# Five barriers between dense stages taken out, with the next stage's first products split by token tile

## The reference

```python
x = x + mix @ w_out                                    # mix_out
hf = causal_dwconv(rms_norm(x, norm2_g) @ w_up, ...)   # up, 1024 -> 2 x 2816
gt, val = split(hf)
x = x + (gelu(gt) * val) @ w_down                      # down
gate = sigmoid(rms_norm(x, norm3_g) @ w_pg)            # gate
x = x + (p @ w_pe) * gate
x = rms_norm(x, final_g)
# second block, layer 0 (even): its input product, attention, experts
x @ even_w_in                                          # even_in
x = layer_norm(ALPHA * x + attention @ w_o, ...)
x = layer_norm(ALPHA * x + routed_moe(x), ...)         # combine0
# layer 1 (odd)
x @ odd_w_in                                           # odd_in
```

## Time and profile before

| | |
|---|---|
| median of 3 runs | 2108.26 us (2101.0 to 2108.62) |
| the profiled execution | 2099.9 us, its span 2098.1 us |
| mean granted TensorE clock | 0.956 of full speed |
| PE busy | 1959.4 us, 93% of the span |
| DVE busy | 671.2 us, 32% |
| ACT busy | 401.1 us, 19% |
| POOL busy | 82.0 us, 4% |
| moved by DMA | 335.56 MB, mean 160 GB/s |

### The profile page before, as it was taken

One profiled execution on the slowest core, in us unless ns is written; L12 is line 12 of the kernel. 1 busy time (PEld: TensorE's weight loads), 2 busy tenths in 40 slices (PEclk: granted clock), 3 DMA queues, 4 the chain that ended last, 5 costly groups with the idle time before them and its releaser, 6 DMA issues.

```text
span 2098.1 us, 23209 instructions
## 1 busy us (share of the span) xinstructions
PE 1959.4 (93%) x9718; PEld 879.6 (42%) x9718; DVE 671.2 (32%) x1600; ACT 401.1 (19%) x869; POOL 82.0 (4%) x106
## 2 busy tenths in 40 slices
PE   7999999999999988999996999998998997999997
PEld 3464444444444444444544333233644445333332
DVE  4736321223200223015534000014776635200005
ACT  3213011111100003105601111112125521111111
POOL 0000010000000000000001100010000000200001
PEclk9989999999999999998996999999989997999999
DMA  4103552221221122201135999992110243799995
GB/s 157 63 21 111 195 195 80 80 74 42 75 80 60 60 80 94 80 1 41 47 139 176 325 399 397 395 390 89 41 40 1 81 161 125 219 397 396 398 388 203
DMA packets 140633, 335.56 MB, mean 160 GB/s; under 512 B 4536, under 2 KB 12744, under 8 KB 140400
## 3 DMA queue, kind: packets, MB, share of 16 engines
q1 hardware_dynamic: 126384, 283.80, 37.3%
q0 software_dynamic: 10976, 37.76, 4.8%
q10 hardware_dynamic: 3168, 12.50, 1.5%
HBM read 310.94 MB, written 23.09 MB: 159 GB/s over the span
## 4 chain that ended last, share of the span: by engine, by line
PE 85%; DMA 6%; DVE 5%; ACT 2%; issue 1%; DVEq 0%; another core or an unknown queue 0%; ACTq 0%; SPq 0%
PE psum L582 39%; PE psum L982 20%; PE psum L825 7%; DMA ring<-in_moe_w_up 5%; PE psum L762 4%; PE psum L894 3%; PE psum L923 2%; PE psum L907 2%; PE psum L1076 1%; PE psum L963 1%; PE psum L594 1%; PE psum L704 1%; ACT ring L1434 1%; PE psum L1007 0%; PE psum L658 0%
## 5 line engine op out<-in xcount | busy, mean ns | idle before, releaser
L982 PE MATMUL psum<-ring,scratch 128*32 128x512 f32 x3840 | 515.5, 603 | 12.8 <-DMA ring<-in_moe_w_up 9.8
L582 PE MATMUL psum<-xT,ring 128*128 128x512 f32 (+2 forms) x1056 | 465.0, 601 | 8.5 <-PE psum L582 3.5
L582 PEld LDWEIGHTS psum<-xT,ring 128*128 128x128 f32 (+2 forms) x1056 | 199.4, 190 | 271.6 <-issue 270.7
L982 PEld LDWEIGHTS psum<-ring,scratch 128*32 128x32 f32 x3840 | 142.8, 111 | 299.0 <-issue 294.8
L582 PE MATMUL psum<-ring,xT 128*128 128x512 f32 (+4 forms) x704 | 240.2, 498 | 2.5 <-ACTq L1185 1.6
L582 PEld LDWEIGHTS psum<-ring,xT 128*128 128x128 f32 x704 | 120.4, 194 | 120.4 <-issue 112.2
L825 PE MATMUL psum<-ring,scratch 128*128 128x512 f32 x352 | 152.7, 594 | 4.0 <-remote 3.3
L1598 DVE SCALAR_TENSOR_TENSOR scratch<-psum,overlay,scratch 128x511 f32<-128x511 f32 x88 | 65.9, 749 | 230.8 <-ACT scratch L1364 229.3
L982 PE MATMUL psum<-xT,scratch 128*32 128x512 f32 x768 | 130.1, 606 | 9.6 <-DMA ring<-in_moe_w_up 9.6
L2135 DVE TENSOR_TENSOR scratch<-psum,scratch 128x512 f32<-128x512 f32 x24 | 16.6, 691 | 337.0 <-PE psum L982 337.0
L762 PE MATMUL psum<-xT,ring 128*128 128x512 f32 x224 | 103.0, 616 | 2.5 <-DVEq L1587 2.3
(11 more groups left out here) (374 smaller groups left out, 1650.4 us busy)
## 6 DMA issues: line engine op xcount, KB each, us to landing
ring<-in_moe_w_gate SPq DMA_DIRECT2D x28, 2048.0 KB, 15.6
ring<-in_moe_w_up SPq DMA_DIRECT2D x28, 2048.0 KB, 18.4
ring<-in_moe_w_down SPq DMA_DIRECT2D x24, 2048.0 KB, 15.1
ring<-in_w_up SPq DMA_DIRECT2D x11, 2048.0 KB, 7.9
xT<-in_moe_w_down SPq DMA_DIRECT2D x8, 2048.0 KB
expert_rows<-scratch ACTq DMA_DIRECT2D x20, 512.0 KB, 7.3
ring<-in_w_down SPq DMA_DIRECT2D x4, 2048.0 KB, 7.8
ring<-in_even_w_in SPq DMA_DIRECT2D x4, 2048.0 KB, 7.8
```

Source lines behind the costliest of these rows:

```text
L582: mm = nc.tensor.matmul(out_, lhsT, rhs, start=(j == 0), stop=(j == len(pairs) - 1))
L982: mm = nc.tensor.matmul(bank[r, :], lhsT[:, t, r], w_[:, t, c0:c0 + 512], start=(t == 0), stop=(t == nk - 1))
```

## The change

NO_MEET gets five stages more: mix_out, up, down, gate and combine0, so the barriers behind them are gone. In their place:

- up, even_in and odd_in begin with enter_features. It waits until tile 2 is in xT, does product 0 for the first 384 tokens, turns tile 3, does product 1 for 384 tokens, waits for tile 3 in xT and does both products for the last 128 tokens. turn_behind leaves tile 3 to it in mix_out, down and gate; combine turns three tiles only.
- down begins as soon as its weights and the first eight hidden tiles are there; each of its first four products waits for one of DVE's last four convolutions.
- gate begins with tile 0 when that is in xT, and turns tile 3 behind its first pair. Its pairs of banks start at bank 4 (gate_bank).
- the stages get semaphores of their own that are never cleared (out_mm, out_used, gate_mm, gate_opened, gate_used, late_taken); static and expert loads into a slot share one semaphore. The remaining Flow sets are cleared behind norm1 and even_in.
- GpSimd now waits in gate for the end of down, then for tile 3, ahead of its two loads, and in odd_in for the late sums ahead of its clearing. Its zero fill, pT load and the memset of qB no longer stand behind barriers.

```diff
-NO_MEET = ("even_out", "route0", "experts0", "overflow0", "odd_out", "route1", "experts1", "overflow1")
+NO_MEET = ("mix_out", "up", "down", "gate", "combine0", "even_out", "route0", "experts0", "overflow0", "odd_out", "route1", "experts1", "overflow1")
...
-        flow = {s: turns[i % 2] for i, s in enumerate(STAGES)}
+        flow = {"norm1": turns[0], "up": turns[1], "even_in": turns[0], "odd_in": turns[1], "latent": turns[0]}
+        done_with = {"norm1": turns[0:1], "even_in": turns}
...
+        def gate_bank(i):
+            return (2 * i + 4) % 8
...
                     turn_tile(stage, n - 1)
+                    if stage in ("mix_out", "down", "gate"):
+                        return
...
+            def tile_there(stage, n):
+                pe.wait_ge(tile_taken, norm_base[stage] + n + 1)
+                if stage == "combine0":
+                    pe.wait_ge(late_taken, n + 1)
+
+            def enter_features(behind, f, columns):
+                def part(k, q):
+                    w_, c0, m = columns[k]
+                    return product(banks[k][0:m, q], [(w_[:, t, c0:c0 + m], xT[:, t, q]) for t in range(KD)])
+                early, last = slice(0, (NT - 1) * P), slice((NT - 1) * P, T)
+                tile_there(behind, NT - 2)
+                part(0, early)
+                turn_tile(behind, NT - 1)
+                part(1, early)
+                tile_there(behind, NT - 1)
+                for k in range(2):
+                    part(k, last).then_inc(f.mm, 1)
...
             def down():
...
+                    pe.wait_ge(val_scaled, k0 + c[2])
                     for n in range(NT):
+                        if j == 0:
+                            pe.wait_ge(F["up"].v, 2 * FT - 3 + n)
...
             def gate():
...
+                        i = NT * half_ + n
+                        if half_ == 0:
+                            tile_there("down", n)
+                        else:
+                            pe.wait_ge(gate_used, i - NT + 1)
...
+                        if i == 0:
+                            turn_tile("down", NT - 1)
...
             def gate():
+                pool.wait_ge(out_mm, OUT_MM["down"] + 24)
                 pool.dma_start(rowsG, w["final_g"]).then_inc(rows_loaded, 16)
+                pool.wait_ge(tile_taken, norm_base["down"] + NT)
                 pool.dma_start(pack_area["even"], w["pack_even"]).then_inc(pack_loaded["even"], 16)
...
             def odd_in():
+                pool.wait_ge(late_done, NT)
                 clear_halves(kI)
```

More of the change, by code:

```diff
@@ L265, in build @@
         met = sem("met")
-        w_loaded = [sem(f"w_loaded{s}") for s in range(RING)]
+        w_loaded = [sem(f"w_loaded{s}") for s in range(RING + 1)]
         w_used = sem("w_used")
@@ L317, in build @@
         for l in range(2):
+            for b in slot_of[len(chunk_loads):first_expert_chunk[l]]:
+                buffer_loads[b] += 1
+                chunk_loads.append(buffer_loads[b])
             holder = {b: (i - RING - 1, None) for i, b in enumerate(FIRST_FREE[l])}
@@ L452, in build @@
         y_taken = sem("y_taken")
-        expert_loaded = [sem(f"expert_loaded{b}") for b in range(RING + 1)]
         y_stored = [sem("y_stored0"), sem("y_stored1")]
@@ L471, in turn_bank @@
         def turn_bank(stage, n):
-            return 2 * n if stage in ("gate", "combine0") else 2 * (n % 2)
+            if stage == "gate":
+                return gate_bank(n)
+            return 2 * n if stage == "combine0" else 2 * (n % 2)
+        def gate_bank(i):
+            return (2 * i + 4) % 8
         keys_cleared = sem("keys_cleared")
@@ L808, in up @@
                     w_ = slot_view(at, c)
-                    for g in range(4):
+                    if j == 0:
+                        enter_features("mix_out", f, [(w_, g * P, P) for g in range(2)])
+                    for g in range(0 if j else 2, 4):
                         k = 4 * j + g
@@ L865, in even_in @@
                     arrived(at)
+                    if j == 0:
+                        enter_features("gate", f, [(slot_view(at, c), g * P, P) for g in range(2)])
+                        k = 2
                     if j == 1:
@@ L971, in weights_of @@
                     b, loads = buffer_of[l][m, e]
-                    pe.wait_ge(expert_loaded[b], loads)
+                    pe.wait_ge(w_loaded[b], loads)
                     views.append(expert_buffer(b, 4 if m == "down" else KD))
@@ L1079, in combine @@
                 if l == 0:
-                    for n in range(NT):
+                    for n in range(NT - 1):
                         turn_tile("combine0", n)
@@ L1371, in gate @@
             def gate():
-                f = F["gate"]
                 def opened(i):
-                    act.wait_ge(f.mm, 2 * i + 2)
+                    act.wait_ge(gate_mm, i + 1)
                     if i >= 2:
-                        act.wait_ge(f.v, i - 1)
-                    A(gate_s[:, i % 2, :], banks[(2 * i + 1) % 8][:, :], ACT.Sigmoid).then_inc(f.a, 1)
+                        act.wait_ge(gate_used, i - 1)
+                    A(gate_s[:, i % 2, :], banks[gate_bank(i) + 1][:, :], ACT.Sigmoid).then_inc(gate_opened, 1)
                 for i in range(NT):
@@ L2329, in _, with meet @@
             steps = [2]
-            def meet(i):
+            def meet(stage):
                 meets[0] += 1
@@ L2335, in meet @@
                 pool.drain()
-                if i >= 0:
-                    f = turns[i % 2]
+                for f in done_with.get(stage, ()):
                     for s in (f.mm, f.a, f.v, f.s):
@@ L2488, in _ @@
             }
-            for i, s in enumerate(stages):
+            for s in stages:
                 if s in run:
@@ L2557, in load_experts @@
                             sp.wait_ge(met, meets_through("odd_d" if l else "even_ab"))
-                    sp.dma_start(expert_buffer(b, 4 if m == "down" else KD), views[m][e]).then_inc(expert_loaded[b], 16)
+                    sp.dma_start(expert_buffer(b, 4 if m == "down" else KD), views[m][e]).then_inc(w_loaded[b], 16)
             for at, c in static:
```

70 lines of the change are left out of this document (34 added, 36 removed).

## The result

| | before | after |
|---|---|---|
| median | 2105.65 us (2101.0 to 2108.62, 4 runs) | 2085.99 us (2083.75 to 2086.48, 4 runs) |
| ratio after / before | | 0.9907, 95% interval 0.9883 to 0.9930 |
| the profiled execution, its span | 2099.9, 2098.1 us | 2086.48, 2084.8 us |
| mean granted TensorE clock | 0.956 | 0.958 |
| PE busy | 1959.4 us | 1957.5 us |

A forecast was written before the change was run, and what follows sets the result against it. TensorE, busy in 93% of the span, bounds the kernel, so only its idle or slow time can be won. Gains of 0.6 + 3.1 + 8.8 + 1.6 + 1.6 = 15.7 us from the 2108.26 median give 2092.6 us, range 2083 to 2099.

The forecast's parts named there:

- into up: Split entry from mix_out into up: PE starts after tile 2's copy, at 266.05 instead of 268.31; gain 0.6 us.
- up to down: Barrier gap of 3.27 us between up and down shrinks to a 0.14 us weight-chunk change; gain 3.1 us.
- inside down: Down's own products: no term in the sum; the new waits are for DVE's convolutions 41 + n.
- down to gate: Gate starts once tiles 1 and 2 are turned, tile 3 behind pair 0, clock full; gain 8.8 us.
- into even_in: Split entry into even_in: PE starts at 823.75 instead of 825.82, restart 2.5 us; gain 1.6 us.
- into odd_in: Split entry into odd_in: PE starts at 1441.9 instead of 1444.37, restart 2.5 us; gain 1.6 us.
- The clock stays up: Rival: no clock fall at the three split entries, sum 23.4 us, time 2084.9 us; chance 0.10.
- Three entries give nothing: Rival: split entries into up, even_in, odd_in gain nothing; only 11.9 us remain, 2096.4 us; chance 0.17.
- Given back in the experts: Rival: earlier PE only waits longer for expert weights; 0 gained, 2108 us; chance 0.08.
- The zero fill starves mix_out: Rival: zero-fill stores delay w_out's second chunk in mix_out; at 155 GB/s 26 us lost, 2118.6 us; chance 0.03.

The follow-up runs named there:

- e6_fewer_waits: Changed kernel with down's wait on val_scaled issued only at the first two weight chunks; 2092.95 us, beside 2093.77 for the unedited changed kernel.
- after_again: The changed kernel unedited, run again on another chip; 2093.77 us against 2115.11 for the kernel before, ratio 0.9893.
- e1_gate_barrier: Changed kernel with the barrier between down and gate put back and tile 3 turned ahead of it; 2091.73 us, ratio 0.9944 to before.
- e3_warm: Changed kernel with dummy 128x128x512 products while PE waits at the entries into up, even_in and odd_in; 2080.24 us, ratio 0.9881 to before.

## Why the prediction was right, and where its sizes were off

The time, 2086.0, lies 6.6 us under the forecast of 2092.6 and inside the range of 2083 to 2099, and faster by over 0.5% was the likeliest case. 2.6 of the 6.6 us come from the reference: I subtracted from a median of 2108.26, and with one more run it is 2105.65. The other 4.0 are a gain of 19.7 where I had 15.7. In the traces the sum came close. By its terms, against the first trace of before:

| join | forecast | measured |
|---|---|---|
| into up | 0.6 (0 to 3.1) | 1.2 |
| up to down | 3.1 (3.0 to 3.2) | 3.0, and 3.0 more where the clock fell |
| inside down | 0 | -0.75 |
| down to gate | 8.8 (8.6 to 8.9) | 9.0, and 7.9 against each of the other two traces |
| into even_in | 1.6 (1.1 to 4.1) | 1.4 |
| into odd_in | 1.6 (1.1 to 4.1) | 1.4 |
| sum | 15.7 | 15.2 |

1.9 us of the 15.2 are missing in the span of the first pair of traces; they lie in stages without a changed join, where executions of one kernel differ by more than that. No trace shows where the 4.0 us beyond the sum lie. Over three traces of before and two of after the sum is 15.8, almost the 15.7 forecast, but that is partly luck, as its terms miss both ways: up to down 1.9 us and into up 0.9 more than forecast, against 0.9 less into odd_in, 0.75 lost inside down, 0.5 less into gate and 0.4 less into even_in.

- **Up to down is the mis-sized term.** I priced the gap at its idle time, 3.27 us, with a bound of 3.0 to 3.2, because in the one trace that I had the clock stood at 1.00 behind it. I had written that a gap has two prices, its idle time and the restart, and did not apply it to the shortest gap. In two further traces the restart was there: 3.0 us. The bound should have been 3.0 to 6.2. Averaged over three traces the term is 3.0 + 2.0 = 5.0.
- **A wait was not costed.** "What stays is a change of weight chunk, 0.14 us of issue" is 0.29, and so is each of the five changes of chunk inside down, instead of 0.14: 0.75 us lost there. I named what the new waits wait for and not that the instruction itself is issued at six chunk changes. e6_fewer_waits gives 0.6 back by dropping four.
- **Into up** was worth 1.2, not 0.6. The start came where I had it to 0.1 us (265.27, against 266.05 less the 0.88 us by which mix_out started earlier). The 16 instructions took 7.09, 1.7 us above full clock where I had 2.5; in after_again they took 7.73, so part of this is the execution. Into even_in and odd_in 7.91 and 7.51 are 2.5 and 2.2 above, as forecast. In the two traces without the split it is likewise worth least into up.
- **Down to gate** went by its steps: tiles 1 and 2 turned from 731.03, product at once, clock 1.00 through the first pair, tile 3 behind it; its copy on DVE ends at 743.75 (L1708), and the next product on PE did not wait for it. e1_gate_barrier gives the same join 7 to 8 us in the trace, and the second and third trace of before 7.9: the bound of 8.6 to 8.9 was too narrow, since it took over from one trace the point at which the clock fell.

The rivals. *The clock stays up* failed at all three entries (0.61, 0.50, 0.50). The Trainium skill, in "TensorE: Matmul & The Clock Gate", section "HAM oscillation", has idle holes of a few microseconds put the clock down, and the prediction leaned that way; the 4.5 and 4.3 us holes agree, and so does e3_warm, which filled them. The hole of 3.27 us between up and down went both ways, so for that size the section's rule is not one by which a single execution can be priced. *Three entries give nothing*: they gave 4.0 us in the first pair of traces, some 3 by the traces without the split; falls, though into up alone it nearly holds. *Given back in the experts* falls: PE's waits for their weights are 17.1 us against 19.4, and SP's waits for PE and ACT are 334.4 and 123.8 us, as in the earlier trace rows; they moved along. *The zero fill starves mix_out* falls: DMA moved 417 GB/s from 215 to 230, above the 382 by which I had costed it, and w_out's second chunk was there at 230.

## What to carry to other kernels

When a barrier is taken out, list what each engine's queue still holds ahead of the tile that the next stage wants: here the first version won 21.3 us, and another 13.7 (with the fewer waits) were left behind because the copies of finished tiles stood behind the last tile's norm. Price a gap on TensorE twice, as idle time and as the half-clock stretch behind it; where a trace shows a gap without that stretch, keep the stretch in the bound, and take a second trace if one can be had. Compare stages between traces only against the scatter of the same stage in a second execution of the same kernel.

## What the runs showed of the hardware that was not expected

- The same gap of 3.27 us, same place and same work on both sides, was followed by a clock of 1.00 in one execution and by 0.50 for some 6 us in two. The gap of 2.84 us into odd_in with early copies went both ways too, and so did the one of 3.34 to 3.35 us ahead of tile 3's turn into up: its eight transposes took 1.86, 1.06 and 1.94 us in the three traces of before. Behind single gaps of 1.4 and 1.8 us (early copies) the clock stayed at 1.00 in both traces that have them. The length of the last gap alone does not tell it: before has gaps of 1.38, 1.48 and 1.80 us ahead of even_in, up and odd_in, each close behind another, and 0.50 to 0.51 behind all three. Behind those of 4.3 and 4.5 us it fell in every trace.
- The granted clock falls to 0.50 without idle time in a stretch of 64 instructions with four columns each, at a different instruction from one execution to the next (8.4 to 11.5 us for the same 64), and a 128x128x512 product between groups of 16 did not prevent it in one execution.
- A satisfied semaphore wait that follows another one on PE takes 0.15 us out of the stream of products.
- The mixers ahead of every changed stage took 201.4 to 206.8 us over the traces of all versions, by execution and not by kernel.
